# Weighted values over the first 128 keys: one float32 product, or three float32r products of high and low parts

## What is computed

```python
p = jnp.exp(s - m[..., None])
o = jnp.einsum('brnhqk,brnkhd->brnqhd', p, vv) / ...      # first block, kind "1"
return jnp.einsum('bhqk,bkhd->bqhd', p.astype(v.dtype), v)  # second block, kinds "A", "B", "C"
```

## Time and profile before

| | us |
|---|---|
| median of 3 runs | 3112.31 |
| the runs | 3112.29 to 3113.07 |
| the profiled execution | 3113.07 |
| its span, first to last instruction | 3111.1 |
| PE busy | 3089.6 (99%) |
| DVE busy | 2128.2 (68%) |
| ACT busy | 1732.5 (56%) |

### The profile page before, as it was taken

How to read it: one execution, slowest core, us unless ns; L and a number is a source line. 1 busy time by engine, 2 the same in 40 slices (tenths; PEclk the granted TensorE clock), 3 DMA queues, 4 the chain that set the end, 5 groups by cost and what they waited for, 6 DMA issues and landing times.

```text
span 3111.1 us, 52092 instructions
## 1 busy us (share of the span) xinstructions
PE 3089.6 (99%) x18230; PEld 2729.8 (88%) x18230; DVE 2128.2 (68%) x2741; ACT 1732.5 (56%) x2291; POOL 0.2 (0%) x4
## 2 busy tenths in 40 slices
PE   9999999999999999999999999999999999999999
PEld 7888888888888788888888888888888888888888
DVE  7677576666667687766766656777776776655675
ACT  5685444444445556656565555645665656555563
POOL 0000000000000000000000000000000000000000
PEclk9999999999999999999999999999999999999999
DMA  7656665555556555565556666566556555666655
GB/s 231 195 173 201 203 190 167 185 178 174 186 168 212 181 172 164 159 202 175 176 174 195 188 183 184 185 201 190 160 159 204 173 179 171 194 190 184 182 186 179
DMA packets 569813, 571.73 MB, mean 184 GB/s; under 512 B 26352, under 2 KB 565488, under 8 KB 569712
## 3 DMA queue, kind: packets, MB, share of 16 engines
q1 hardware_dynamic: 569712, 570.42, 59.3%
HBM read 568.25 MB, written 2.10 MB: 183 GB/s over the span
## 4 chain that ended last, share of the span: by engine, by line
PE 94%; DVE 3%; ACT 1%; issue 1%; DMA 0%; SPq 0%; DVEq 0%; ACTq 0%
PE pg L536 89%; PE pa L780 1%; PE pa L797 1%; DVE hl L1285 1%; PE pa L787 1%; PE pa L536 1%; PE pa L753 1%; ACT hl L942 1%; PE pa L798 1%; PE pa L710 0%; DMA raw<-w_in 0%; DVE uT L1366 0%; PE pa L888 0%; DVE gat L1373 0%; DVE xres L1744 0%
## 5 line engine op out<-in xcount | busy, mean ns | idle before, releaser
L536 PE MATMUL pg<-hT,hl 128*128 128x512 f32 x11456 | 1995.2, 334 | 1.2 <-DVE hl L1285 1.2
L536 PEld LDWEIGHTS pg<-hT,hl 128*128 128x128 f32 x11456 | 1730.7, 188 | 227.6 <-DVE hl L1285 2.4
L1285 DVE TENSOR_TENSOR hl<-raw,hl 128x1024 fp32r<-128x1024 f32 (+1 forms) x1071 | 1254.5, 1209 | 298.6 <-ACT hl L942 290.8
L942 ACT ACTIVATE hl<-raw 128x1024 fp32r<-128x1024 f32 (+1 forms) x1071 | 1084.6, 1044 | 294.0 <-PE pg L536 274.0
L536 PE MATMUL pg<-uT,hl 128*128 128x256 f32 (+1 forms) x3712 | 629.9, 331 | 15.9 <-DVE uT L1366 7.4
L536 PEld LDWEIGHTS pg<-uT,hl 128*128 128x128 f32 x3712 | 554.2, 189 | 87.0 <-issue 14.8
L950 ACT ACTIVATE corr<-pg 128x512 f32<-128x512 f32 x286 | 170.0, 594 | 819.5 <-PE pg L536 819.5
L536 PE MATMUL pg<-hl,hT 128*128 128x512 f32 (+1 forms) x1792 | 318.5, 336 | 0.0
L536 PEld LDWEIGHTS pg<-hl,hT 128*128 128x128 f32 x1792 | 274.5, 188 | 38.6
L1292 DVE TENSOR_TENSOR work<-pg,corr 128x512 f32<-128x512 f32 (+1 forms) x154 | 105.8, 687 | 293.3 <-ACT corr L950 292.9
L1117 ACT ACTIVATE work<-work,sm 128x256 f32<-128x256 f32 (+3 forms) x144 | 69.3, 482 | 131.2 <-DVE sm L1563 129.2
(11 more groups left out here) (191 smaller groups left out, 1370.7 us busy)
## 6 DMA issues: line engine op xcount, KB each, us to landing
raw<-w_in SPq DMA_DIRECT2D x791, 512.0 KB, 4.7
raw<-w_br SPq DMA_DIRECT2D x96, 512.0 KB, 4.4
raw<-w_out SPq DMA_DIRECT2D x64, 512.0 KB, 4.9
raw<-w_rnn SPq DMA_DIRECT2D x32, 512.0 KB, 4.9
raw<-w_o SPq DMA_DIRECT2D x32, 512.0 KB, 5.1
raw<-w_att SPq DMA_DIRECT2D x16, 512.0 KB, 4.0
raw<-w_uq SPq DMA_DIRECT2D x16, 384.0 KB, 4.0
tab<-tabs SPq DMA_DIRECT2D x5, 896.0 KB, 7.4
```

The costliest lines, as they stand in the source:

```text
L536: return nc.tensor.matmul(out, lhsT, rhs, start=start, stop=stop, skip_group_check=True)
L942: nc.scalar.activation(part(j, 0, h, 0, n), raw[:, bass.ds(j % 2 * UC + a, n)], ACT.Copy)\
L1285: tt(part(j, 1, h, 0, n), raw[:, bass.ds(j % 2 * UC + a, n)], part(j, 0, h, 0, n).bitcast(F32), ALU.subtract).then_inc(lo_done, 1)
```

## The change

The product over the first 128 keys (L797) becomes `three_terms` of a high and a low part of the values and of the transposed probabilities. The product over the second 128 keys stays float32. The parts are made so:

- ACT, new event `v0`: copies the first half of the values as float32r, the high part. DVE, new event `v0`: values minus high part, the low part (`v_hi`, `v_lo`).
- ACT, event `t`: the one copy out of PSUM becomes two, one of the columns of the second keys and one of the 256 queries against the first keys, rounded to float32r. DVE, new event `y`: PSUM minus the high part (`pt_lo`).
- PE waits for `v_lo` once per pair and for `pt_lo` where it waited for `pt_ready`: before the weighted values, before the second head's scores in kind "1" and before its transposes in kind "B".

`mix_r` and a new `work_r` are views of memory that other tiles use at other times.

```diff
 ACT_EVENTS = EVENTS | {
-    "1": events("u0-11") + EVENTS["1"],
-    "A": events("u0 q0 u1 q1 u2 h6 norm h7-8 s0-1 h9-10 t0-1 h11 p0-1"),
-    "B": events("u0-4 norm u5-6 s0 u7-8 t0 s1 u9 p0 h20 t1 h21 p1 h22 n0-1 h23 o0-1"),
+    "1": events("u0-15 s0 u16-17 t0 u18 v0 s1 u19-20 p0 t1 u21 p1 u22-23"),
+    "A": events("u0 q0 u1 q1 u2 h6 norm v0 h7-8 s0-1 h9-10 t0-1 h11 p0-1"),
+    "B": events("u0-4 norm u5-6 v0 s0 u7-8 t0 s1 u9 p0 h20 t1 h21 p1 h22 n0-1 h23 o0-1"),
+    "C": events("u0-4 norm u5-6 v0 s0-1 u7-8 t0-1 u9 p0 u10 p1 u11"),
 }
 DVE_EVENTS = {
-    "1": events("... u13-15 s0 x0 u16-18 s1 x1 u19-20 p0 u21 lo0 p1 u22 lo1 u23"),
-    "A": events("u0 q0 u1-2 h6 rot norm h7-8 s0-1 x0-1 h9-11 p0-1 lo0-1"),
-    "B": events("u0-4 norm rot u5-6 s0 x0 u7-8 s1 x1 u9 h20-22 n0-1 h23 lo0-1"),
-    "C": events("u0-4 norm u5-6 s0-1 x0-1 u7-9 p0 u10 lo0 p1 lo1 u11"),
+    "1": events("... u13-15 s0 x0 u16-17 y0 u18 v0 s1 x1 u19-20 p0 y1 u21 lo0 p1 u22 lo1 u23"),
+    "A": events("u0 q0 u1-2 h6 rot norm h7 v0 h8 s0-1 x0-1 h9-10 y0-1 h11 p0-1 lo0-1"),
+    "B": events("u0-4 norm rot u5-6 v0 s0 x0 u7-8 y0 s1 x1 u9 h20 y1 h21-22 n0-1 h23 lo0-1"),
+    "C": events("u0-4 norm u5-6 v0 s0-1 x0-1 u7-8 y0-1 u9 p0 u10 lo0 p1 lo1 u11"),
 }
...
             def weighted_values(kind, e):
...
                 for m in range(nm):
                     pt = transposed(kind, e)[1][:, m, :]
-                    va, vb = (v_1[:, t, m, es] if kind == "1" else v_l[:, t, es] for t in range(2))
-                    nc.tensor.matmul(weighted(kind, e), va, pt[:, 0:S], start=m == 0, stop=False, skip_group_check=True)
-                    ins = nc.tensor.matmul(weighted(kind, e)[:, P:S], vb, pt[:, S:SM], start=False, stop=m == nm - 1,
-                                           skip_group_check=True)
+                    vb = v_1[:, 1, m, es] if kind == "1" else v_l[:, 1, es]
+                    three_terms(out, vh[:, m, es], vl[:, m, es], ph[:, m, :], pl[:, m, :], m == 0, False)
+                    ins = mm(out[:, P:S], vb, pt[:, S:SM], False, m == nm - 1)
...
                         if j and kind == "1":
-                            pe.wait_ge(pt_ready, 2 * pi + 1)
+                            pe.wait_ge(pt_lo, 2 * pi + 1)
                         scores(kind, j)
...
                         if j and kind == "B":
-                            pe.wait_ge(pt_ready, 2 * pi + 1)
+                            pe.wait_ge(pt_lo, 2 * pi + 1)
                         transposes(kind, j)
                     elif what == "p":
-                        pe.wait_ge(pt_ready, 2 * pi + j + 1)
+                        if j == 0:
+                            pe.wait_ge(v_lo, pi + 1)
+                        pe.wait_ge(pt_lo, 2 * pi + j + 1)
                         weighted_values(kind, j)
...
-                        nc.scalar.activation(dst, src, ACT.Copy).then_inc(pt_ready, 1)
+                        nc.scalar.activation(dst[:, :, S:], src[:, :, S:], ACT.Copy)
+                        nc.scalar.activation(pt_split(kind, j)[0], src[:, :, 0:S], ACT.Copy).then_inc(pt_ready, 1)
+                    elif what == "v":
+                        act.wait_ge(evac_done, c + (11 if kind == "1" else 5))
+                        nc.scalar.activation(v_split(kind)[0], v_first(kind), ACT.Copy).then_inc(v_hi, 1)
...
+                    elif what == "y":
+                        high, low = pt_split(kind, j)
+                        dve.wait_ge(pt_ready, hd + 1)
+                        tt(low, transposed(kind, j)[0][:, :, 0:S], high.bitcast(F32), ALU.subtract).then_inc(pt_lo, 1)
+                    elif what == "v":
+                        high, low = v_split(kind)
+                        dve.wait_ge(v_hi, pi + 1)
+                        tt(low, v_first(kind), high.bitcast(F32), ALU.subtract).then_inc(v_lo, 1)
```

More of the change, by code:

```diff
@@ L80 @@
 ACT_EVENTS = EVENTS | {
-    "1": events("u0-11") + EVENTS["1"],
-    "A": events("u0 q0 u1 q1 u2 h6 norm h7-8 s0-1 h9-10 t0-1 h11 p0-1"),
-    "B": events("u0-4 norm u5-6 s0 u7-8 t0 s1 u9 p0 h20 t1 h21 p1 h22 n0-1 h23 o0-1"),
+    "1": events("u0-15 s0 u16-17 t0 u18 v0 s1 u19-20 p0 t1 u21 p1 u22-23"),
+    "A": events("u0 q0 u1 q1 u2 h6 norm v0 h7-8 s0-1 h9-10 t0-1 h11 p0-1"),
+    "B": events("u0-4 norm u5-6 v0 s0 u7-8 t0 s1 u9 p0 h20 t1 h21 p1 h22 n0-1 h23 o0-1"),
+    "C": events("u0-4 norm u5-6 v0 s0-1 u7-8 t0-1 u9 p0 u10 p1 u11"),
 }
 DVE_EVENTS = {
-    "1": events("u0-2 rot0 u3-4 rot1 u5-6 rot2 u7-8 rot3 u9-10 rot4 u11-12 rot5 u13-15 s0 x0 u16-18 s1 x1 u19-20 p0 u21 lo0 p1 u22 lo1 u23"),
-    "A": events("u0 q0 u1-2 h6 rot norm h7-8 s0-1 x0-1 h9-11 p0-1 lo0-1"),
-    "B": events("u0-4 norm rot u5-6 s0 x0 u7-8 s1 x1 u9 h20-22 n0-1 h23 lo0-1"),
-    "C": events("u0-4 norm u5-6 s0-1 x0-1 u7-9 p0 u10 lo0 p1 lo1 u11"),
+    "1": events("u0-2 rot0 u3-4 rot1 u5-6 rot2 u7-8 rot3 u9-10 rot4 u11-12 rot5 u13-15 s0 x0 u16-17 y0 u18 v0 s1 x1 u19-20 p0 y1 u21 lo0 p1 u22 lo1 u23"),
+    "A": events("u0 q0 u1-2 h6 rot norm h7 v0 h8 s0-1 x0-1 h9-10 y0-1 h11 p0-1 lo0-1"),
+    "B": events("u0-4 norm rot u5-6 v0 s0 x0 u7-8 y0 s1 x1 u9 h20 y1 h21-22 n0-1 h23 lo0-1"),
+    "C": events("u0-4 norm u5-6 v0 s0-1 x0-1 u7-8 y0-1 u9 p0 u10 lo0 p1 lo1 u11"),
 }
@@ L202, in build @@
         xres = sb("xres", NT * S)
-        with nc.sbuf_tensor("mix_r", [P, 10 * S], F32R) as mix_r:
+        with nc.sbuf_tensor("mix_r", [P, 12 * S], F32R) as mix_r:
+            pt_lo_a = [mix_r[:, (10 + e) * S:(11 + e) * S].unsqueeze(1) for e in range(2)]
             sq_a = [mix_r[:, 5 * S * h:5 * S * h + 5 * S].rearrange("p (t n) -> p t n", n=S) for h in range(2)]
@@ L212, in build @@
         sm = sb("sm", 200)
+        with nc.sbuf_tensor("work_r", [P, 31 * 256 + 128], F32R) as work_r:
+            vl_1 = work_r[:, 18 * S:21 * S].rearrange("p (g n) -> p g n", g=3)
+            vl_l = work_r[:, 24 * S:25 * S].unsqueeze(1)
+            pt_hi_1 = work_r[:, 27 * 256:27 * 256 + 1152].rearrange("p (m n) -> p m n", m=3)[:, :, 0:S]
+            pt_hi_l = [work_r[:, a:a + S].unsqueeze(1) for a in (27 * 256 + 768, 2 * S)]
         work = sb("work", 31 * 256 + 128)
@@ L288, in build @@
                              "pv_done"))
+        v_hi, v_lo, pt_lo = sem("v_hi"), sem("v_lo"), sem("pt_lo")
         o_ready, o_hi, u_ready = sem("o_ready"), sem("o_hi"), sem("u_ready")
@@ L353, in transposed, with pt_split, v_split, v_first @@
             return pa3[:, 0:1, 0:SM], nt3[:, 2:4, :].rearrange("p t n -> p (t n)")[:, 0:SM].unsqueeze(1)
+        def pt_split(kind, e):
+            if kind == "1":
+                return pt_hi_1, uT[:, 10 * 512:10 * 512 + 768].rearrange("p (m n) -> p m n", m=3)
+            one = kind == "B" or e == 0
+            lo = pt_lo_a[e] if kind == "A" else (u3[:, 12, S:] if one else u3[:, 13, 0:S]).unsqueeze(1)
+            return pt_hi_l[0 if one else 1], lo
+        def v_split(kind):
+            if kind == "1":
+                return uT[:, 8 * 512:8 * 512 + 768].rearrange("p (g n) -> p g n", g=3), vl_1
+            return u3[:, 14 if kind == "A" else 12, 0:S].unsqueeze(1), vl_l
+        def v_first(kind):
+            return v_1[:, 0, :, :] if kind == "1" else v_l[:, 0:1, :]
         def weighted(kind, e):
@@ L793, in weighted_values @@
                 nm = 3 if kind == "1" else 1
+                out = weighted(kind, e)
+                vh, vl = v_split(kind)
+                ph, pl = pt_split(kind, e)
                 for m in range(nm):
                     pt = transposed(kind, e)[1][:, m, :]
-                    va, vb = (v_1[:, t, m, es] if kind == "1" else v_l[:, t, es] for t in range(2))
-                    nc.tensor.matmul(weighted(kind, e), va, pt[:, 0:S], start=m == 0, stop=False, skip_group_check=True)
-                    ins = nc.tensor.matmul(weighted(kind, e)[:, P:S], vb, pt[:, S:SM], start=False, stop=m == nm - 1,
-                                           skip_group_check=True)
+                    vb = v_1[:, 1, m, es] if kind == "1" else v_l[:, 1, es]
+                    three_terms(out, vh[:, m, es], vl[:, m, es], ph[:, m, :], pl[:, m, :], m == 0, False)
+                    ins = mm(out[:, P:S], vb, pt[:, S:SM], False, m == nm - 1)
                 ins.then_inc(pv_done, 1)
```

## The result

The change makes the kernel slower: 3137.04 us (median of 6 runs) against 3113.31 us, a ratio of 1.0075 with a 95% interval from 1.0065 to 1.0085. The direction was forecast, the size was not: 23.7 us where I had worked out 8.8, above my range.

What follows compares the result with a forecast made beforehand. The prediction took PE, busy 99% of the span, as the bound. From the 3112.3 us median, 5.0 us gained by triples and 13.8 us of kind B waits gave 3121.1 us, range 3114.5 to 3125.0.

Steps and rivals of the forecast that it cites:

- part 4: Added ACT and DVE work in kinds A, C and 1 is covered before PE needs it and costs nothing.
- a PE instruction saved in the attention is worth its full time: Opening step: with PE busy 99% of the span, PE time saved or waited in the attention counts in full.
- The wait in kind B: PE's p1 in kind B waits for y1, 1.73 us late per pair; 8 pairs, 13.8 us.
- order alone: Rival: only y1's place behind three low-part subtractions in kind B counts, 1.05 us per pair; 3115.7 us, chance 0.12.
- The chain's shift: In kind B, v0 ahead of s0 and y0 ahead of s1 each delay the chain 0.34 us, together 0.68 us.
- The triple: Three float32r matmuls take 0.36 us against 0.43 us for the product replaced; 72 products gain 5.0 us.
- Kinds A, C and 1 don't wait: No idle before their weighted values; the rival with waits in A and 1 had 3127 us, chance 0.10.
- The clock did not fall in kind B: Rival: waits around t1 and p1 of each B pair lower PE's granted clock; 3141 us, chance 0.02.
- All covered: Rival: the waits on y1 never bite, so only the 5.0 us gain remains; 3107.3 us, chance 0.11.
- four passes to three: Rival: a float32r matmul costs a quarter of 0.43 us; 3118.2 us with waits, 3104.4 us all covered; chance 0.03.

Runs made afterwards that it cites:

- float32_in_the_middle: Changed kernel with the float32 product of the second keys moved between the first and second term of the triple: 3122.75 us, ratio 1.0031 to the kernel before.
- b_order: Changed kernel with three VectorE events of kind B moved: v0 and y0 behind the row maxima, y1 ahead of the third low-part subtraction: 3124.15 us, ratio 1.0035.
- v0_y0_in_gaps: Changed kernel with only v0 and y0 of kind B moved into gaps where VectorE waits for exponentials; y1 left behind three subtractions: 3132.28 us.
- order_and_middle: Changed kernel with three VectorE events of kind B moved and the float32 product between the triple's first and second term: 3108.13 us, ratio 0.9984.
- low_probs_in_work: Changed kernel with the low part of kind C's probabilities in work, where the high part lies, instead of uT: 3130.11 us, ratio 1.0052.

## Why the prediction was wrong

The term that failed is one that I did not write: part 4 gave every place outside the weighted values a price of nothing, and the sum took the weight stream behind them at its pace of before. That stream is over 90% of PE's time, and by the count above it lost some 15.5 us. With the waits still in and nearly all of the added slow stretches gone, float32_in_the_middle took 3122.75 us, 1.7 us above the forecast of 3121.1. The step that let it through stands at the start: "a PE instruction saved in the attention is worth its full time". It holds only while the matmuls around it keep their distance (the time from start to start). The trace before had both paces in it, 81 matmuls in 14 us behind 970 us and 84 in 14 us behind 996 us:

```profile
970.00:984.00 14.00, 14.00 (x81) 12.27 (x81) 11.65 (x13) 7.39 (x9) 0.00 (x0) 1.00 1.04 346
996.00:1010.00 14.00, 14.00 (x84) 12.42 (x83) 9.41 (x11) 8.42 (x13) 0.00 (x0) 1.00 0.63 208
```

The slow one of the two also has more DMA traffic (346 against 208 GB/s), but from 520 to 580 us the slow stretch has less of it (187 against 194), so the traffic does not set the pace there. The distances of single matmuls, read there, would have shown a risk of both signs, with a bound: some 3% of the stream.

The steps that I did write held:
- *The wait in kind B.* Forecast 1.73 us from p0 to p1, measured 1.72; forecast 1.05 for the order alone, measured 1.06. Over 8 pairs 13.8 forecast. b_order took 12.9 us off the median, 13.7 off the two B stages.
- *The chain's shift.* 0.34 us each for v0 and y0, measured 0.33. Two operations in two gaps of 1.9 us cost nothing (v0_y0_in_gaps).
- *The triple.* 0.36 us forecast and measured: in kind 1 the first map's triple begins at 503.81 and its float32 product at 504.17.

```profile
503.81 0.28 PE L562 MATMUL pa<-work_r,uT 128*128 128x256 f32 x1
...
504.17 0.38 PE L562 MATMUL pa<-work 128*128 128x128 f32 x2
```

"FP8 and Floating Point Precision" of the Trainium skill, section "TensorE Precision Notes", has four passes for a true float32 product; the estimate from it was three quarters of 0.43 us, 0.32. The trace doesn't bear the estimate out: in triples a float32r matmul of 256 columns takes 0.12 us from start to start here, not 0.11. The gain was 5.2 us with both repairs in, 5.0 forecast; as order_and_middle still has 1.6 us of added slow pace, that agreement is partly luck.
- *Kinds A, C and 1 don't wait.* No such row in the waits. The clock did not fall in kind B: granted 1.00 in both its stages.
- *All covered* and *order alone* fell with the 16 new waits; *four passes to three* with the row above.

What stays open: why the operand's place matters. Shown is that in kind C moving the low probabilities from `uT` to `work` removes the slow pace and moving them inside `uT` does not, that the order of four matmuls decides, and that one more turned tile inside a slow stretch ends it. How PE's weight loads and reads of moving data lock into one rhythm or the other is not shown by any run. In kind 1 leaving out either low part removes it, so there it takes both; moving its operands was not tried.

## What to carry to other kernels

Where one engine is full, compare not only its waits but the distances of its instructions in stretches that the change does not touch: 3% there outweighed all that was computed about the edited place. An operation of 0.4 us added to an engine that is busy two thirds of the time is free or costs its consumer 1 us, by its place in the queue alone; put it into a gap in which that engine waits anyway, and ahead of work that nobody needs yet. When an edit on PE loses time that no wait explains, reorder its few matmuls before giving it up.

## What the runs showed of the hardware

I had not expected that a stream of weight loads and float32r matmuls has two steady paces at a granted clock of 1.00: 340 and 350 ns for a pair of 512 and 256 columns. It keeps the one it fell into, for up to the 448 matmuls of one stretch, until a turned tile or a change of operands interrupts the pattern. Which one it falls into hangs on a few matmuls ahead of the stream: on their order (float32_in_the_middle), and in kind C on where one operand of one of them lies (low_probs_in_work). "TensorE: Matmul & The Clock Gate" of the Trainium skill, section "Wait — 56ns, not 53.3ns?", gives the columns divided by 2.4 GHz plus about 2.5 ns between starts. An estimate from it is 325 ns for such a pair; neither pace of this kernel is that fast.
